# A two-layer decoder trunk with weights split into two parts: straight code instead of loops, and raw and low weight parts in one ring of six slots

## The reference

```python
c_act = silu(c)
for layer in range(2):
    if layer == 1:   # one shared K/V set for the second attention
        k_sh, v_sh = shared_kv(x, c_act, kv_ada_w, kv_ada_b, kv_norm_g, kv_w_k, kv_w_v, ...)
    shift_t, scale_t, gate_t, shift_m, scale_m, gate_m = split(c_act @ ada_w[layer] + ada_b[layer])
    h = rms_norm(x, norm_g[layer, 0]) * (1 + scale_t) + shift_t
    y = mixer_a(h, ...) if layer == 0 else mixer_b(h, k_sh, v_sh, ...)
    x = x + gate_t * y
    h = rms_norm(x, norm_g[layer, 1]) * (1 + scale_m) + shift_m
    x = x + gate_m * (square(relu(h @ w1)) @ w2)
```

## Time and profile before

| | us |
|---|---|
| median of 3 runs (lowest, highest) | 2616.8 (2614.7, 2618.7) |
| profiled execution, own time | 2620.6 |
| its span, first to last instruction | 2618.9 |
| TensorE busy | 2417.1 (92%) |
| VectorE busy | 1871.4 (71%) |
| ScalarE busy | 1149.8 (44%) |
| DMA, mean over the span | 254 GB/s |
| TensorE's mean granted clock | 0.974 |

### The profile page before, as it was taken

One profiled execution on the slowest core, in us unless ns is written; L12 is line 12 of the kernel. 1 busy time (PEld: TensorE's weight loads), 2 busy tenths in 40 slices (PEclk: granted clock), 3 DMA queues, 4 the chain that ended last, 5 costly groups with the idle time before them and its releaser, 6 DMA issues.

```text
span 2618.9 us, 30970 instructions
## 1 busy us (share of the span) xinstructions
PE 2417.1 (92%) x10901; PEld 1972.1 (75%) x10901; DVE 1871.4 (71%) x2285; ACT 1149.8 (44%) x1766; POOL 65.7 (3%) x128
## 2 busy tenths in 40 slices
PE   0399999998899999999998988988899999999999
PEld 0288888876787888888886876777687888788887
DVE  7788786977788677677776867877796555555554
ACT  1255445454543443443445454454543343343442
POOL 1100000000100000000001010000100000000000
PEclk9599999999899999999998999999899999999999
DMA  9777685866788777787785866766696555555554
GB/s 365 282 283 293 218 338 209 345 246 235 278 299 323 267 279 263 287 293 259 276 308 182 311 225 266 298 223 241 267 366 210 192 186 186 169 185 185 192 179 158
DMA packets 150355, 665.66 MB, mean 254 GB/s; under 512 B 16752, under 2 KB 17104, under 8 KB 120784
## 3 DMA queue, kind: packets, MB, share of 16 engines
q1 hardware_dynamic: 150224, 663.95, 69.4%
HBM read 661.78 MB, written 2.10 MB: 253 GB/s over the span
## 4 chain that ended last, share of the span: by engine, by line
PE 76%; DVE 14%; issue 5%; ACT 4%; DMA 2%; POOL 0%; SPq 0%; DVEq 0%; ACTq 0%
PE main L384 24%; PE main L386 24%; PE main L385 24%; DVE acc L930 5%; DVE w_lo L911 4%; PE tr L397 2%; ACT w_hi L676 1%; DVE st_a L995 1%; PE tr L439 1%; DMA w_raw<-w 1%; DMA qT<-ada 1%; ACT st_b L702 1%; PE tr L451 0%; ACT sm L733 0%; DMA ada_raw<-ada 0%
## 5 line engine op out<-in xcount | busy, mean ns | idle before, releaser
L676 ACT ACTIVATE w_hi<-w_raw 128x1024 fp32r<-128x1024 f32 x800 | 845.5, 1060 | 1306.5 <-PE main L386 1102.8
L911 DVE TENSOR_TENSOR w_lo<-w_raw,w_hi 128x1024 fp32r<-128x1024 f32 x800 | 974.7, 1225 | 571.5 <-ACT w_hi L676 570.1
L384 PE MATMUL main<-w_hi,hT_hi 128*128 128x512 f32 x2176 | 873.8, 402 | 7.2 <-DVE hT_lo L1093 4.0
L385 PE MATMUL main<-w_lo,hT_hi 128*128 128x512 f32 x2176 | 853.6, 392 | 3.3 <-issue 3.3
L386 PE MATMUL main<-w_hi,hT_lo 128*128 128x512 f32 x2176 | 853.4, 392 | 0.0
L384 PEld LDWEIGHTS main<-w_hi,hT_hi 128*128 128x128 f32 x2176 | 413.3, 190 | 94.8 <-DVE w_lo L911 5.0
L386 PEld LDWEIGHTS main<-w_hi,hT_lo 128*128 128x128 f32 x2176 | 412.4, 190 | 91.8 <-issue 3.5
L385 PEld LDWEIGHTS main<-w_lo,hT_hi 128*128 128x128 f32 x2176 | 413.3, 190 | 84.1 <-issue 1.5
L930 DVE SCALAR_TENSOR_TENSOR acc<-ada_raw,c_act,acc 128x2048 f32<-128x2048 f32 x194 | 455.1, 2346 | 12.5 <-DMA ada_raw<-ada 11.0
L384 PE MATMUL main<-w_hi,mid_hi 128*128 128x512 f32 x1024 | 405.8, 396 | 0.0
L386 PE MATMUL main<-w_hi,mid_lo 128*128 128x512 f32 x1024 | 403.7, 394 | 0.0
(11 more groups left out here) (159 smaller groups left out, 1124.8 us busy)
## 6 DMA issues: line engine op xcount, KB each, us to landing
w_raw<-w SPq DMA_DIRECT2D x800, 512.0 KB, 4.2
ada_raw<-ada SPq DMA_DIRECT2D x208, 1024.0 KB, 6.2
qT<-ada SPq DMA_DIRECT2D x16, 1024.0 KB, 7.4
gate<-bias_rows SPq DMA_DIRECT2D x4, 1024.0 KB, 6.9
xs<-x SPq DMA_DIRECT2D x1, 2048.0 KB, 9.7
out<-xs SPq DMA_DIRECT2D x4, 512.0 KB, 5.0
gains_sb<-gains SPq DMA_DIRECT2D x1, 640.0 KB, 4.5
st_a<-lamb SPq DMA_DIRECT2D x1, 256.0 KB, 5.3
```

What stands on the lines that cost most here:

```text
L384: pe.matmul(acc_ps[:, :], hi[:, kt, tc], w_hi[:, s, wc], start=(kt == 0), stop=False)
L385: pe.matmul(acc_ps[:, :], hi[:, kt, tc], w_lo[:, s, wc], start=False, stop=False)
L676: act.activation(w_hi[:, s, :], w_raw[:, s, :], ACT.Copy).then_inc(hi_done, 1)
L911: dve.tensor_tensor(w_lo[:, s, :], w_raw[:, s, :], w_hi[:, s, :].bitcast(F32), ALU.subtract).then_inc(lo_done, 1)
```

## The change

Three things are changed together.
1. `repeat` and the counters' loop bases go; each loop is written out by Python, so that every wait is on a constant and every DMA address is fixed. Gains and mask are read where they lie; `gain_now` and `mask_now` and their copies go.
2. `SLOTS` is 6. `w_lo` is declared and given up ahead of `w_raw`, so both have the same address: VectorE subtracts in place. `w_raw` / `w_lo` and `w_hi` are two rings of six slots, 48 KB as before.
3. The waits follow: SyncE issues piece n when the matmuls of piece n-6 are done (`mm_done`); ScalarE waits for the landing alone; VectorE and TensorE wait as before.

The core of the diff (all other places only drop the loop base from a wait):

```diff
-SLOTS = 4
+SLOTS = 6
...
+        with nc.sbuf_tensor("w_lo", [P, SLOTS, PK * NC], F32R) as w_lo:
+            pass
         w_raw = sb("w_raw", [P, SLOTS, PK * NC])
         w_hi = sb("w_hi", [P, SLOTS, PK * NC], F32R)
-        w_lo = sb("w_lo", [P, SLOTS, PK * NC], F32R)
...
-        gain_now = sb("gain_now", [P, 2 * HD])
-        mask_now = sb("mask_now", [P, 3 * P], BF16)
...
                 s = (n["w"].n - 1) % SLOTS
-                sp.wait_ge(lo_done, n["w"]())
-                at = n["w"](n["w"].n - 1)
-                src = wv[at] if isinstance(at, int) else wv[bass.ds(at, 1), :, :].rearrange("a p c -> p (a c)")
-                sp.dma_start(w_raw[:, s, :], src).then_inc(raw_in[s], 16)
+                sp.wait_ge(mm_done, n["w"].n)
+                sp.dma_start(w_raw[:, s, :], wv[n["w"].n - 1]).then_inc(raw_in[s], 16)
...
-            with repeat(sp, GROUPS - 1, n, ada=KT, w=6 * PIECES):
+            for _ in range(GROUPS - 1):
                 for ch in range(6):
                     chunk(ch, ada=ADA_QKV)
...
-                    pe.wait_ge(lo_done, n["w"](n["w"].n + SLOTS))
+                    pe.wait_ge(lo_done, n["w"].n)
...
                 block(0)
-                with repeat(pe, 2, n, **rises):
-                    block(None)
+                for number in (1, 2):
+                    block(number)
                 block(3, True)
...
                 n["w"].up()
-                w, base = n["w"].n, n["w"].base
-                s = (w - 1) % SLOTS
-                fills = ((w - 1) // SLOTS + 1) * 16
-                act.wait_ge(raw_in[s], fills if base is None else base * (16 // SLOTS) + fills)
-                act.wait_ge(mm_done, n["w"]())
+                fills, s = divmod(n["w"].n - 1, SLOTS)
+                act.wait_ge(raw_in[s], 16 * (fills + 1))
                 act.activation(w_hi[:, s, :], w_raw[:, s, :], ACT.Copy).then_inc(hi_done, 1)
...
-            dve.sem_inc(lo_done, SLOTS)
...
-                dve.tensor_copy(gain_now[:, 0:HD], q_gain)
-                dve.tensor_copy(gain_now[:, HD:2 * HD], k_gain)
-                chained(dve.tensor_copy(mask_now[:, :], mask))
```

More of the change, by code:

```diff
@@ L82, in __missing__ @@
         return self[name]
[L85 to L97, removed]
 def cols(i, size):
-    return slice(i * size, (i + 1) * size) if isinstance(i, int) else bass.ds(i * size, size)
+    return slice(i * size, (i + 1) * size)
 def after(*lists, first=0):
@@ L328, in _ @@
                 chunk(ch, ada=ADA_GATE + ADA_FIRST)
-            with repeat(sp, 2, n, ada=KT, w=8 * PIECES):
+            for _ in range(2):
                 for ch in range(8):
@@ L344, in _ @@
                 chunk(ch, ada=ADA_GATE_B)
-            with repeat(sp, 2, n, w=8 * PIECES):
+            for _ in range(2):
                 for ch in range(8):
@@ L569, in group @@
                     gemm(0, *h, side=also(attn_a(1, 1)[0], halves(sum_columns, 1)))
-            with repeat(pe, GROUPS - 1, n, ada=KT, w=6 * PIECES, ro0=3, ro1=3, roped=4, tr0=10, tr1=10, sc=8,
-                        p=8, ov=4):
+            for _ in range(GROUPS - 1):
                 group(False)
@@ L686, in ended @@
             def ended(back):
-                act.wait_ge(mm_done, n["w"](n["w"].n + SLOTS - back))
+                act.wait_ge(mm_done, n["w"].n + SLOTS - back)
             def chained(ins):
@@ L831, in group @@
                     chunk(PIECES, {4: [values(1)], 8: [exps(True)]})
-            with repeat(act, GROUPS - 1, n, w=6 * PIECES, seq=4, qk=8, smx=2, pt=8):
+            for _ in range(GROUPS - 1):
                 group(False)
@@ L874, in mlp @@
                 block()
-                with repeat(act, 2, n, w=8 * PIECES, mid=8, x=4):
+                for _ in range(2):
                     block()
@@ L1136, in ended @@
             def ended(back):
[L1138 removed]
+                dve.wait_ge(mm_done, n["w"].n + SLOTS - back)
             def update(c, back=4):
@@ L1257, in _ @@
             dve.wait_ge(consts, 3)
-            with repeat(dve, GROUPS - 1, n, w=6 * PIECES, ada=KT, landed=KT, col=4, seq=20, rms=4, qk=8, sc=8, pt=8, ov=4) as g:
+            for g in range(GROUPS - 1):
                 group(g, False)
             group(GROUPS - 1, True)
+            sc4 = [mask_scores(m, masks[:, GROUPS - 1, :]) for m in range(MAPS)]
             lows = [low_of_heads(j) for j in range(PIECES)]
@@ L1301, in block @@
                     sides += [{4: [update(c)]} for c in range(3)]
-                    first = isinstance(i, int) and i == 0
+                    first = i == 0
                     if first:
@@ L1310, in block @@
                         chunk(7, PIECES, {4: [update(3)]})
-                rises = dict(w=8 * PIECES, relu=4, mid=8, hi=8, seq=8)
-                if ada:
-                    rises.update(ada=KT, landed=KT, col=4, seq=9)
-                block(0)
-                with repeat(dve, 2, n, **rises) as i:
-                    block(i + 1)
-                block(3, True)
+                for i in range(4):
+                    block(i, i == 3)
             mlp([], (S_SCALE_M0, S_SHIFT_M0), 1, ADA_MLP, ADA_GATE + ADA_FIRST, DRAIN + len(ADA_WO), 2)
```

91 lines of the change are left out of this document (38 added, 53 removed).

## The result

Before 2617.7 us (median, 2614.7 to 2619.0), after 2593.8 us (2592.3 to 2596.0); ratio 0.9906, 95% interval 0.9893 to 0.992. That is 24 us less, where the forecast said 17 less (2599.6 us); the range of 2589 to 2613 holds it.

The account below looks back on a forecast made before the run. TensorE, busy 92% of the span, bounds the kernel, with weight supply ahead nearly everywhere. Gains 6.1 + 6.4 + 3.6 + 1.1 = 17.2 us from the median 2616.8 give 2599.6 us; own range 2597 to 2609, 80% range 2589 to 2613.

Parts of the forecast that it names:

- back edge: TensorE's loop over the second MLP's middle blocks, hole at 2268 us: writing it out gives back 6.1 us.
- four turns: Turns into both MLPs, q0 and key/value: earlier splits let the updates start sooner, 6.4 us in all, bounds 2.1 to 8.4.
- four attention chunks: Three groups and one key/value chunk: split goes ahead, statistics chain starts 0.9 us earlier, 3.6 us in all.
- head pair: Chunk after the last attention unit: split no longer delays the last head pair's high part, 1.1 us, bounds 0 to 1.2.
- starvation: TensorE stopping for weight pieces because transfers are issued later; loss put at 0.
- rule of the Trainium skill: Instruction fetch at taken branches: each of TensorE's three back edges would pay, 18 us; the sum kept 6.1.
- My own formula: At the turns: issue 0.27, landing, split plus subtraction 2.29 us, set against issue two pieces (5.6 us) before the end.
- In place, same room: Raw and low part sharing a slot, VectorE subtracting in place: worth 0, bounds +-2 ns on 800 subtractions.
- What is lost: Transfers run six pieces ahead of TensorE instead of up to eight; loss put at 0.
- slower rival: Transfers starve TensorE at four turns, up to 34 us, 2633 us; chance 0.09.
- rival on `mid`'s step: Moving buffers 1792 bytes may turn the 0.2333 us step of `mid` matmuls: 19 us more gain, 2580.6 us; chance 0.07.

Follow-up runs that it names:

- one loop: Kernel before with only TensorE's loop over the second MLP's middle blocks written out: 2612.0 us beside 2618.1, ratio 0.9974.
- turns held: Kernel after with the old split wait back at four places, the fourth split after each turn: 2605.3 us, ratio 0.9946 against the kernel before.
- mid_moved: Kernel after with 64 unused bytes ahead of `mid`, to a multiple of 128 bytes: 2594.0 us, ratio 0.9901 against the kernel before.
- mid_first: Kernel after with `mid` placed ahead of all other buffers: 2576.9 us, ratio 0.9836 against the kernel before.
- hT_last: Kernel after with the places of `hT` and `mid` exchanged: 2605.4 us, ratio 0.9944 against the kernel before.
- loops alone: Kernel before with all engines' loops written out, rings untouched (also loops_only): 2611.7 us beside 2619.7, ratio 0.997.
- split held: Kernel after with ScalarE's split again waiting for the matmuls four pieces back: 2610.9 us, ratio 0.9968 against the kernel before.
- raw8_high4: Kernel after with eight raw/low and four high slots, split waiting four pieces back: 2611.6 us, ratio 0.9975 against the kernel before.

## Why the prediction was right, step by step

The right column is the difference of the two profiled executions, by TensorE's chunks; the runs that stand behind it are named.

| step | forecast | found |
|---|---|---|
| back edge | 6.1 | 6.4 (one loop: 6.4 in the trace, 6.0 in the medians) |
| four turns | 6.4 | 8.5 (turns held: 8.6 in the trace) |
| four attention chunks | 3.6 | 4.5 (1.05, 1.03, 1.01 in the groups, 1.45 in key/value) |
| head pair | 1.1 | 1.2 |
| groups' first chunks | - | 2.1 |
| starvation | 0 | -1.7 |
| key/value chunks 2 to 7 | - | 4.2 |
| small, everywhere | - | 1.5 |
| sum | 17.2 | 26.7 |

The forecast of 17.2 us was right in its mechanisms and too small; 24 us were measured by the medians. Nearly 6 of the 26.7 us of the traces (key/value chunks and "small") are given to no cause, so how near the medians came to the forecast is partly luck.

*The edge.* Right in place and size. I had weighed a rule of the Trainium skill against it ("Runtime: NRT & Kernel Launch", "Instruction fetch mechanics"), by which all three back edges of TensorE would pay. The one-loop kernel still has the two others and is as fast as the one with none: here one edge of three costs. Why that one does, no run shows. VectorE's edge, put at nothing, was worth 0.3 us.

*The turns.* The mechanism was right, the size too small. The term that was mis-sized is the landing: I had an unloaded 3.4 us and the run's 4.2, and took the middle; for the second MLP I even let 7.4 us in. In after, the fourth piece landed in 4.31, 3.29, 3.31 and 3.24 us. My own formula with these numbers gives 0.27 + landing + 2.29 - 5.6 = 1.3, 0.2, 0.3 and 0.2 us late, and 1.40, 0.22, 0.40 and 0.33 were measured. The row to take for the two middle turns was that of the unloaded stretch: in the four kernels where the split goes ahead with six slots (after, mid_moved, mid_first, hT_last) this piece landed in 3.25 to 3.42 us there. For the first and the last turn the wider bounds were right: it took 3.23 to 4.31 and 3.14 to 4.21 us, and with 4.21 (mid_moved) the gain into the second MLP was 1.3 us, just what I had taken. The 2.25 of after are the lucky end. The key/value turn gained 0.5 us more than its subtraction; that was not followed up.

*The attention chunks.* 0.9 us forecast, 1.0 found. I had looked for the pattern (fourth split in front of the statistics, TensorE waiting at the chain's end) only in the fourth chunk of a group. The first chunk has it too (in the second group of after its fourth split starts 0.66 us ahead of the chunk's first matmul, with loops alone 0.26 behind it, and the statistics follow the split): 27.32 us with loops alone and with the split held, 26.69 after, in the second and third group. That is 1.3 of the 2.1 us; the rest of it goes with the loops. The groups' first chunks were a term put at nothing without a reason.

*In place, same room.* Nothing, as forecast: split_held has both and equals loops alone.

*What is lost.* Forecast 0, found 1.7 us at one place in this execution. The slower rival named the right danger (adaLN pieces crowding the queue, landings of 8 us) but the wrong stretch, 1905 to 1965; there the ring's lead held. What it did not have is how a short ring costs most: with four slots, 41 waits for pieces make 40.7 us; in the one chunk followed above, 10 us go to the order behind the fourth split, which I had not counted at all. How the other 150 us divide between this order and the slower clock was not counted.

*The key/value section.* 4.2 us of the difference are in its chunks 2 to 7, where I forecast nothing. They can't be given to the change: three kernels that hold every split (loops_only, split_held, raw8_high4) have 187.8, 191.1 and 189.2 us there in their profiled executions, before 191.2; turns_held, in which these chunks are as in after, has 190.5 where after has 187.0. The third chunk of the section alone goes from 32.7 to 35.9 us among the kernels that hold the split. What sets them stayed open.

*The rival on `mid`'s step.* It did not happen (44.8 us for two chunks before and after), but the place was the cause, as it supposed, and there were 17 us in it (mid_first against after). The 1792 bytes by which `mid` moved left it in the dear place.

## What to carry to other kernels

An in-order engine that prepares operands ahead of use and also does the work at a turn makes each wait of the first kind a wait of the second. Before deepening a ring for bandwidth, look at what stands behind the instruction that waits for a slot: the gain was there (16 us), and in the supply six slots against four with the split held brought none that could be told. The depth follows from it: the piece in front of the turn's work must be issued a landing plus a split plus a subtraction (here 6 us, over two pieces) before the turn; one slot less made the kernel slower than the old one.

With a fixed room, try to divide it by lead: seven slots for the ring that waits for transfers and five for the one that waits for an engine were better than six and six in both pairs here, by 4 and 9 us, though with overlapping intervals.

## What the hardware showed

- The same matmuls (128 x 128 stationary, 512 columns, clock 1.00) step at 0.2333 or 0.2267 us by the place of the stationary operand. Counted in each partition from the first buffer, by the sizes in the kernel, the cheap places were 0 to 32 KB (`mid` in mid_first), 112 to 144 KB (`hT` in after) and 144 to 176 KB (`hT` in mid_first), the dear one some 174 to 206 KB (`mid` in after, `hT` in hT_last). What in the address matters is open, and so is whether the distance to other buffers does.
- One back edge of TensorE of three stood 3.3 us and cost 6 in all, the lower clock behind it included; VectorE's stood 3.6 to 4.5 us and was hidden but for 0.3.
- A 512 KB weight piece that was issued just ahead of a turn landed in 3.1 to 3.4 us in most cases and in 4.2 to 4.4 at some of the first and last turns (kernels in which the split goes ahead), and in 8.2 us (median) with five 1 MB pieces around it.
